# The first layer's projection and its mixing in one stage, part of the conditioning moved to the feed-forward, and one row of the second layer at partition 32

## The reference, cut to what matters

```python
proj = x @ w_in
xa, ba, ca, u, v, xc, da, dg, q, gate = jnp.split(proj, SPLIT_OFFSETS, axis=-1)
y_a = short_gated_conv(xa, ba, ca, conv_a_w)                 # 3 taps
y_b = spatial_gating(u, v, sg_ln_g, sg_ln_b, sg_w, sg_b)     # gelu, layer norm of v, a triangular product over tokens
y_c = multiscale_pool(xc, pool_w, pool_scale)                # trailing means over 2, 4, 8, 16 tokens
y_d = conformer_conv(da, dg, ...)                            # 31 taps, layer norm, silu, a product
y_e = memory_cross_attention(q, mem, w_kv)                   # 4 heads, 256 keys
h = jnp.concatenate([y_a, y_b, y_c, y_d, y_e], axis=-1) * jax.nn.silu(gate)
return h @ w_out
```

## Time and profile before

| what | value |
|---|---|
| median of 3 runs | 2344.21 us (2336.35 to 2350.68) |
| the profiled execution's own time | 2339.87 us |
| its span in the trace | 2338.0 us |
| TensorE, mean granted clock | 0.951 of full |
| TensorE busy | 2187.8 us, 94% |
| VectorE busy | 708.2 us, 30% |
| ScalarE busy | 518.4 us, 22% |
| GpSimd busy | 269.4 us, 12% |

### The profile page before, as it was taken

One profiled execution on the slowest core, in us unless ns is written; L12 is line 12 of the kernel. 1 busy time (PEld: TensorE's weight loads), 2 busy tenths in 40 slices (PEclk: granted clock), 3 DMA queues, 4 the chain that ended last, 5 costly groups with the idle time before them and its releaser, 6 DMA issues. The chain is left out here.

```text
span 2338.0 us, 24977 instructions
## 1 busy us (share of the span) xinstructions
PE 2187.8 (94%) x9866; PEld 1453.9 (62%) x9866; DVE 708.2 (30%) x984; ACT 518.4 (22%) x877; POOL 269.4 (12%) x301
## 2 busy tenths in 40 slices
PE   5999758999999999999999999999999999999992
PEld 3554333665555444444444667675599999999991
DVE  2688631234555200000001366676200000000003
ACT  0000120143432100000001665763112111111110
POOL 2222000200000100000000344443120000000001
PEclk9999868789989999999999999999999999999995
DMA  9887301111110222221321211110196586777863
GB/s 349 307 282 266 137 0 36 36 37 55 54 46 28 72 74 80 74 79 46 121 75 45 64 58 51 55 46 19 67 304 196 185 279 215 247 267 281 297 235 117
DMA packets 81356, 308.66 MB, mean 132 GB/s; under 512 B 9840, under 2 KB 10360, under 8 KB 80992
## 3 DMA queue, kind: packets, MB, share of 16 engines
q1 hardware_dynamic: 60768, 238.05, 30.5%
q0 software_dynamic: 16800, 59.87, 7.2%
q10 hardware_dynamic: 3680, 9.23, 1.1%
HBM read 297.27 MB, written 9.85 MB: 131 GB/s over the span
## 5 line engine op out<-in xcount | busy, mean ns | idle before, releaser
L243 PE MATMUL banks<-sb_x_norm,sb_ring 128*128 128x512 f32 x1344 | 597.3, 604 | 3.9 <-ACT sb_x_norm L385 3.9
L1836 PE MATMUL banks<-sb_act,sb_ring 128*128 128x128 f32 (+3 forms) x4224 | 559.7, 295 | 1.8 <-DVE sb_act L1984 1.0
L1836 PEld LDWEIGHTS banks<-sb_act,sb_ring 128*128 128x128 f32 x4224 | 557.3, 191 | 2.9 <-issue 2.7
L243 PEld LDWEIGHTS banks<-sb_x_norm,sb_ring 128*128 128x128 f32 x1344 | 257.7, 194 | 317.5 <-issue 315.0
L243 PE MATMUL banks<-sb_x_res,sb_ring 128*128 128x512 f32 x448 | 198.7, 603 | 0.0
L1984 DVE TENSOR_TENSOR sb_act<-sb_work,banks 128x128 f32<-128x128 f32 (+3 forms) x88 | 27.7, 315 | 527.4 <-PE banks L1836 527.4
L243 PE MATMUL banks<-sb_act,sb_ring 128*128 128x512 f32 x352 | 153.0, 598 | 3.4 <-PEq L1219 3.4
L243 PEld LDWEIGHTS banks<-sb_x_res,sb_ring 128*128 128x128 f32 x448 | 85.5, 193 | 102.9 <-issue 102.9
L243 PEld LDWEIGHTS banks<-sb_act,sb_ring 128*128 128x128 f32 x352 | 67.5, 192 | 88.9 <-issue 88.9
L538 DVE SCALAR_TENSOR_TENSOR sb_x_norm<-sb_work,sb_cond,sb_x_norm 128x1024 f32<-128x1024 f32 x84 | 107.9, 1284 | 41.2 <-DMA sb_work<-in_cond_w 39.5
L254 PEld LDWEIGHTS banks<-sb_ring,sb_x_norm 128*128 128x128 f32 x1024 | 116.0, 192 | 2.5 <-issue 2.4
(11 more groups left out here) (326 smaller groups left out, 1791.9 us busy)
## 6 DMA issues: line engine op xcount, KB each, us to landing
sb_ring<-in_w_moe_up SPq DMA_DIRECT2D x176, 512.0 KB, 4.5
sb_work<-in_cond_w POOLq DMA_DIRECT2D x96, 512.0 KB, 5.5
sb_ring<-in_w_moe_down SPq DMA_DIRECT2D x64, 704.0 KB, 5.7
sb_ring<-in_w_ffn_up SPq DMA_DIRECT2D x44, 512.0 KB, 3.6
sb_ring<-in_w_h_in SPq DMA_DIRECT2D x32, 512.0 KB, 3.6
sb_ring<-in_w_in SPq DMA_DIRECT2D x28, 512.0 KB, 6.9
sb_ring<-in_w_m_in SPq DMA_DIRECT2D x24, 512.0 KB, 3.6
sb_ring<-in_w_ffn_down SPq DMA_DIRECT2D x16, 704.0 KB, 4.1
```

What stands on the lines that cost most here:

```text
L243: last = m.nc.tensor.matmul(bank[:, 0:act.shape[2]], w[:, rows(k, P)], act[:, k, :], start=(k == 0), stop=(k == kt - 1))
L1836: last = nc.tensor.matmul(ps[:, b % BANKS, 0:cap], m.ring[:, s, rows(k, P)], act, start=(k == 0), stop=(k == kt - 1))
```

## The change

1. `stage_project` and `stage_mix` become `stage_first`. The order of the 28 blocks is DA, DGT, Q, V, U, XC, XA, BA, CA, and the ten gates last. The projection uses two banks in turn (0 and 1); the mixing's products have banks 2 to 6 and stand between the blocks, in an order written out by hand for each engine. Heads are taken in pairs on the two halves of the partitions, and each head of a pair has its own banks and probability tiles. The mixing results go to `W` ungated, and VectorE multiplies each by its gate at the end.
2. Of the twelve conditioning groups, VectorE sums the first, and GpSimd sums groups 1 to 4, with a multiplication and an add per chunk; before, it only issued their loads. The sums of all five go to bank 7. Groups 5 to 11 move to `stage_ffn`: GpSimd issues 56 chunk loads, VectorE adds three chunks after each pair (its loop is unrolled), and TensorE sums over partitions for all seven groups behind the 44 blocks. What the second layers' norm and router need is finished there.
3. In `stage_m` the negated maximum goes to partitions 32 to 39, with a second copy of `sel` there (one more transfer in the setup). `spread_max` of the next head is issued directly behind `spread_floor`, when the exponentials of the present head are done, instead of at the next head's start behind its weights.
4. The masking of `sgw` and the packing of `gates_w` on GpSimd move to the start of `stage_first`.

```diff
@@ Chip.__init__ @@
-        self.sel = sb("sel", [HEADS, HEADS, P])
+        self.sel = sb("sel", [32 + HEADS, HEADS, P])
...
@@ stage_first, replaces stage_project and stage_mix @@
+def spread_group(m, sums, bank, c):
+
+    for j in range(COND // P):
+        last = m.nc.tensor.matmul(m.ps[:, bank, c * 8 + j:c * 8 + j + 1], sums[:, rows(j, P)], m.ones[:, 0:1],
+                                  start=True, stop=True)
+    return last
...
+        @block.gpsimd
...
+            load(0)
+            load(1)
+            pool.wait_ge(m.blocks_done, kv.done + kv.n)
+            load(2)
+            load(3)
+            for n in range(CHUNKS, KD + CHUNKS):
+                pool.wait_ge(chunk_used, n - CHUNKS + 1)
+                load(n)
+            for c in range(1, EARLY_GROUPS):
+                if c >= 2:
+                    pool.wait_ge(acc_done, c - 1)
+                for k in range(KD):
+                    n = c * KD + k
+                    pool.wait_ge(chunk_in[n % CHUNKS], 16 * (n // CHUNKS + 1))
+                    src, total, w = chunk[n % CHUNKS], sums[c % 2], m.cond[:, k:k + 1]
+                    if k == 0:
+                        step(nc.gpsimd.tensor_scalar(total, src, w, None, ALU.mult))
+                    else:
+                        step(nc.gpsimd.tensor_scalar(src, src, w, None, ALU.mult))
+                        step(nc.gpsimd.tensor_tensor(total, total, src, ALU.add))
+                    if n + CHUNKS < EARLY_GROUPS * KD:
+                        load(n + CHUNKS)
+                pool.sem_inc(acc_ready, 1)
...
+            def project(name):
+                b = at[name]
+                s = b % SLOTS
+                pe.wait_ge(m.loaded[s], 16 * (inn.uses[s] + b // SLOTS + 1))
+                pe.wait_ge(m.evac, inn.done + b - 1)
+                by_feature(ps[:, b % 2, :], m.ring[:, s, :]).then_inc(m.blocks_done, 1)
...
+                spread_group(m, sums[c % 2], 7, c).then_inc(acc_done, 1)
...
+            def scores(j):
+
+                pe.wait_ge(m.evac, out_of(Q + 1))
+                if j:
+                    pe.wait_ge(pt_out, 2 * j)
+                for t in range(ST):
+                    for i in range(2):
+                        lo = 64 * i
+                        last = nc.tensor.matmul(ps[:, 2 + 2 * i + t // 2, rows(t % 2, MEM)],
+                                                A[lo:lo + 64, Q + j, rows(t, P)], kT[lo:lo + 64, j, :], start=True,
+                                                stop=True)
+                last.then_inc(score, 1)
...
+            for name in (DA, DA + 1, DGT, DGT + 1, Q, Q + 1):
+                project(name)
+            scores(0)
+            project(V)
+            project(V + 1)
+            turn_probs(0)
+            project(U)
+            attend(0)
+            scores(1)
+            project(U + 1)
+            project(XC)
+            turn_probs(1)
+            project(XC + 1)
+            attend(1)
+            norm_v.mean(m, pe)
+            spread_sums(0)
+            spread_sums(1)
+            project(XA)
+            norm_v.var(m, pe)
+            project(XA + 1)
+            project(BA)
+            turn_values()
+            project(BA + 1)
+            gating()
+            pe.wait_ge(conv_done, 1)
+            norm_c.mean(m, pe)
+            project(CA)
+            norm_c.var(m, pe)
+            project(CA + 1)
+            project(GATES[0])
+            pool_groups()
+            spread_sums(2)
+            project(GATES[1])
+            pointwise()
+            for name in GATES[2:6]:
+                project(name)
+            spread_sums(3)
+            for name in GATES[6:]:
+                project(name)
+            spread_sums(4)
...
@@ scalar, its order @@
+            for name in (DA, DA + 1, DGT, DGT + 1, Q, Q + 1):
+                take(name)
+            exps(0)
+            take(V)
+            take(V + 1)
+            take_probs(0)
+            take(U)
+            take_attended(0)
+            exps(1)
+            take(U + 1)
+            take(XC)
+            take_probs(1)
+            take(XC + 1)
+            take_attended(1)
+            norm_v.square(m, act)
+            take(XA)
+            norm_v.root(m, act)
+            take(XA + 1)
+            take(BA)
+            act.wait_ge(vt_ready, 1)
+            give(act, nc.scalar.activation(A[:, 30:32, :], ps[:, 4:6, :], ACT.Copy), vt_out, 1)
+            take(BA + 1)
+            norm_c.square(m, act)
+            take(CA)
+            norm_c.root(m, act)
+            take(CA + 1)
+            take(GATES[0])
...
@@ vector @@
+            for k in range(KD):
+                dve.wait_ge(chunk_in[k % CHUNKS], 16 * (k // CHUNKS + 1))
+                weigh(m, step, chunk[k % CHUNKS], sums[0], k)
+                dve.sem_inc(chunk_used, 1)
+            dve.sem_inc(acc_ready, 1)
+
+            ready(DGT + 1)
+            step(nc.vector.tensor_tensor(h_in, h_in, A[:, DGT:DGT + 2, :], ALU.mult))
             for f in range(2):
-                step(nc.vector.tensor_scalar(m.conv[:, f, :], h[:, f, :], m.p("dw_w", 2 * (TAPS_D - 1) + f),
+                step(nc.vector.tensor_scalar(conv[:, f, :], h_in[:, f, :], m.p("dw_w", 2 * (TAPS_D - 1) + f),
                                              m.p("dw_b", f), ALU.mult, ALU.add))
-            per = -(-(TAPS_D - 1) // (nch - 3))
-            for c in range(3, nch):
-                conditioning(c)
-                taps(1 + per * (c - 3), min(1 + per * (c - 2), TAPS_D))
-
-            ready(XA)
-            x, s, d = A[:, XC:XC + 2, :], W[:, 12:14, :], A[:, 30:32, :]
-
-            def double(out, src, back):
-                step(nc.vector.tensor_copy(out[:, :, :back], src[:, :, :back]))
-                step(nc.vector.tensor_tensor(out[:, :, back:], src[:, :, back:], src[:, :, :S - back], ALU.add))
-
+            taps(1, 9)
+            softmax(0)
+            taps(9, 16)
+            softmax(1)
+            taps(16, TAPS_D - 1)
...
+            norm_v.centre(m, dve)
+            ready(XC + 1)
+            x, s, d = A[:, XC:XC + 2, :], pooled, pool_tmp
...
+            dve.wait_ge(pw_done, 1)
+            step(nc.vector.tensor_copy(y(YD), ps[:, 4:6, :]))
+            dve.wait_ge(pv_out, 2)
+            for name in GATES:
+                ready(name)
+                tile = W[:, name - GATE, :]
+                step(nc.vector.tensor_tensor(tile, tile, A[:, name, :], ALU.mult))
+            dve.wait_ge(acc_done, EARLY_GROUPS)
+            finish_conditioning(m, step, 0, EARLY_GROUPS, ps[:, 7, 0:8 * EARLY_GROUPS],
+                                ((0, 0, "norm1"), (0, 1, "norm2")))
...
@@ stage_m @@
+    max_row, sel_max, sel_floor = W[32:32 + HEADS, 15, :], m.sel[32:32 + HEADS], m.sel[0:HEADS]
...
+            def spread_max(h):
+                nc.tensor.matmul(ps[:, 5, :], sel_max[:, h, :], max_row, start=True, stop=True).then_inc(spread, 1)
+
             def spread_floor(h):
                 if h:
                     pe.wait_ge(m.norm_in, norms[h - 1].in_k)
                 else:
                     pe.wait_ge(cT_out, 1)
                     pe.wait_ge(floor_out, 1)
-                nc.tensor.matmul(ps[:, 6, :], m.sel[:, h, :], g["f"], start=True, stop=True).then_inc(floor, 1)
+                    pe.wait_ge(row_out, 1)
+                if h < HEADS - 1:
+                    pe.wait_ge(decay, h + 1)
+                nc.tensor.matmul(ps[:, 6, :], sel_floor[:, h, :], g["f"], start=True, stop=True).then_inc(floor, 1)
+                if h < HEADS - 1:
+                    spread_max(h + 1)
...
-                nc.tensor.matmul(ps[:, 5, :], m.sel[:, h, :], g["t"], start=True, stop=True).then_inc(spread, 1)
+                    spread_max(0)
...
@@ stage_ffn @@
+    late = GROUPS - EARLY_GROUPS
+    chunk = [wide(W[:, 2:4, :]), wide(W[:, 4:6, :])] + [wide(A[:, 24 + 2 * i:26 + 2 * i, :]) for i in range(2)]
+    sums = [wide(W[:, 6 + 2 * i:8 + 2 * i, :]) for i in range(6)] + [wide(A[:, 22:24, :])]
...
+            pe.wait_ge(m.acc_ready, GROUPS)
+            for c in range(late):
+                last = spread_group(m, sums[c], 4, c)
+            last.then_inc(m.acc_done, 1)
+
+        @block.gpsimd
+        def _(pool):
+            for n in range(late * KD):
+                if n >= CHUNKS:
+                    pool.wait_ge(m.chunk_used, KD + n - CHUNKS + 1)
+                pool.dma_start(chunk[n % CHUNKS], m.cond_w[EARLY_GROUPS * KD + n]).then_inc(chunk_in[n % CHUNKS], 16)
...
+            def conditioning(n):
+                c, k = divmod(n, KD)
+                dve.wait_ge(chunk_in[n % CHUNKS], 16 * ((EARLY_GROUPS * KD + n) // CHUNKS + 1))
+                weigh(m, step, chunk[n % CHUNKS], sums[c], k)
+                dve.sem_inc(m.chunk_used, 1)
+                if k == KD - 1:
+                    dve.sem_inc(m.acc_ready, 1)
+
+            per = -(-late * KD // (plan.n // 2 - 2))
+            for j in range(plan.n // 2):
+                one(j, j % pairs)
```

(5 more changed lines are left out.)

460 lines of the change are left out of this document (226 added, 234 removed).

## The result

The changed kernel takes 2268.66 us (median of 4 runs, 2266.4 to 2269.22) against 2340.28 us (2335.82 to 2350.68) for the kernel before in the same comparison: ratio 0.9686, 95% interval 0.965 to 0.9722. It is 3.1% faster. The forecast was 2316 us, 1% faster; the measured time lies at the very lower end of the range, where the rival of little contention stood.

What follows compares the result with a forecast made beforehand. TensorE was taken to bound the product stage and later stages, a chain through three engines the mixing. From 2339.87 us, -36 - 1 + 0.7 - 7 + 20 = -23 gave 2316 us, range 2268 to 2333.

Steps and rivals of the forecast that it cites:

- the rival of little contention: Merged stage: GpSimd's multiplication leaves VectorE alone, or the chip arbitrates finer; -79 in the stage, 2273 us, chance 0.22.
- the waits: Merged stage: TensorE waits for VectorE and GpSimd, 0.7 + 18.3 + 4.2 + 21.2 = 44.4 us.
- The merged stage: First layer's product and mixing stages in one: output product starts at 332.4 instead of 368.39, -36 us.
- the second layer: Moved spread_max runs beside spread_floor, saving 1.05 us in seven heads: -7 us, bounds 0 and -20.
- The clock: Merged stage: three restarts at 2.1 us and two falls among the mixing pieces, together 12 us, range 4 to 18.
- TensorE's work: Merged stage: blocks 192.3, five spreads 9.0 and mixing 31 total 232.3 us without any wait.
- the mixing: Merged stage: TensorE's mixing work at full clock, 31 us, with 2.6 taken off for array halves side by side.
- The feed-forward: One-column records behind its product 18 us, VectorE's small operations and a scan 2.5, chunk loads and adds hidden: +20 us.
- The output product: Product behind the merged stage: weights stream in as before, it may keep the clock, -1 us (0 to -2).
- the setup: Kernel's start: one more DMA issue on ScalarE's queue, +0.7 us (0 to 1).
- A cheap multiplication: Merged stage: GpSimd's multiplication costs 1.28 us for 1024 columns, waits shrink to 19; 2291 us, chance 0.07.
- GpSimd ending the stage: Merged stage: GpSimd's 1024-column operations cost 1.3 times the line, last spread waits 21 us; 2355 us, chance 0.07.

Runs made afterwards that it cites:

- c1_mult_broadcast: Changed kernel with GpSimd's multiplication by a column written as a product of two tensors, the second a broadcast column: 2297.74 us, ratio 0.9816.
- a1_no_sums: Changed kernel without GpSimd's arithmetic from the second chunk of each group on, loads and waits kept: 2243.37 us, ratio 0.9577.
- c2_sums_on_vector: Changed kernel with VectorE adding all forty chunks instead of GpSimd, normed values ahead of pooling, spreads where their group is due: 2244.71 us, ratio 0.9598.

## Why the prediction was right and wrong

**The step that failed** is this premise: "an operation of GpSimd is let through between two of VectorE, and VectorE's next one waits until it has ended", applied to the multiplication too ("Nothing shows it for GpSimd's multiplication by a column, the longer one; I assume the same"). It holds for GpSimd's operations that read two tensors: an add of 2.35 us makes a tap 2.72. The multiplication by a column lets VectorE go after some 0.9 of its 2.85 us. With that, four taps pass in a chunk's 6.4 us, 16 taps take 25.5 us, and the waits are 20.4 us instead of 44.4. The merged stage was missed by 35.1 us (-71.1 against -36); 24.0 of them are these waits, and `c1_mult_broadcast`, where the premise holds for both operations, brings 19.7 of them back. Of the whole miss of some 50 us, the second layer has another 10.2 and the third layer's two falls 3.9.

The Trainium skill has both halves of the rule. Trainium Architecture — The Big Picture, What this means for kernel authors, calls the shared port pair of VectorE and GpSimd "an exclusive lock (not a bandwidth split)"; the trace agrees for the adds, behind whose end the held tap finishes (2.72 us for 0.75). Beside a multiplication a tap takes 1.48 us, and the trace does not tell a short stop from a slower run. The Trainium skill's GPSIMD Engine Reference, Key points, names VectorE's instructions with two SBUF inputs, or in a 2-port mode, as those that contend; the taps read two tensors, and the trace agrees, but the runs add that it depends on GpSimd's operation how long they suffer (1.48 us for a tap beside a multiplication, 2.71 beside a product of two tensors).

**The clock**, 12 us by the prediction, cost 4.6. TensorE's records behind the two waits in the changed kernel, and the transposes of `turn_values` in `a1_no_sums`, which does not wait there:

```profile
107.08 1.97 PE L621 MATMUL banks<-sb_cst,sb_act 128*128 128x128 f32 x8 [7.91 <-DVE sb_act L811]
110.43 1.97 PE L621 MATMUL banks<-sb_cst,sb_act 128*128 128x128 f32 x8 [1.38 <-DVE sb_act L811]
112.19 8.21 PE L243 MATMUL banks<-sb_x_res,sb_ring 128*128 128x512 f32 x16
...
186.80 1.97 PE L640 MATMUL banks<-sb_cst,sb_act 128*128 128x128 f32 x8 [10.38 <-DVE sb_act L861]
188.56 7.58 PE L243 MATMUL banks<-sb_x_res,sb_ring 128*128 128x512 f32 x16
```

```profile
166.44 1.04 PE L637 MATMUL banks<-sb_cst,sb_act 128*128 128x128 f32 x8
```

The transposes take twice their time (2.0 us lost in the sixteen ahead of the first block, 0.9 in the eight ahead of the second) and the blocks 8.2 and 7.6 us for 7.0 (1.2 and 0.6 lost). A restart thus cost 2.3 us in the mean, close to the 2.1 of the prediction; there were two instead of three, and no mixing piece made the clock fall in this kernel. In the kernel with waits of 15, 7 and 17 us the stage's mean granted clock was 0.93 instead of 0.96.

**TensorE's work**, 232.3 us without waits by the prediction, is 228.0: in `c2_sums_on_vector`, where the clock is 1.00 throughout, the stretch is 232.0 us with 4.0 us of waits. That the stretches without GpSimd's arithmetic last 232.3 and 232.0 us with their waits is chance. What was too dear is **the mixing**, 26 us at full clock by the starts of its rows, not 31: the halves of the array do work side by side (16 records of scores in 2.00 us, 8 of attending in 1.94, where 0.43 us for 512 columns makes 3.4), which saves 6 us where 2.6 were taken, and the transposes and the gating take 6.3 us instead of 8. The sum of the miss is 24.0 (waits) + 7.4 (clock) + 4.3 (work) = 35.7 us for the 35.1.

**The second layer** was the other mis-sized term: -7, measured -17.2 (-13.2 for the edit alone in the kernel before, with one fall left). The bound of -20, with the four clock falls gone as well, was named, and not taken. The seven pairs saved the 7.4 us that were said of them, but the wait for the exponentials, which was to cost nothing, took 2.1 of it back in three heads; the rest, 11.9 us, is the falls'.

**The feed-forward**, +20, was right in sum (+19.3), with two terms that cancel. The one-column records took 20.5 us (18 forecast). The small operations, 2.5 by estimate, cost nothing: the gap ahead of the down product is 3.1 us, against 3.4 before, because they stand where VectorE's last product stood, and that one now runs under the one-column records. The chunks' loads and adds were hidden, as said. **The output product** (-1) and **the setup** (+0.7) were within 1.3 us.

**The rivals.** Little contention was forecast at 2273 with a chance of 0.22, and the time came out there, but only its first sentence holds, that the multiplication leaves VectorE alone, and that in part: the time landed at 2268 because the second layer gave 10 us more, while 20.4 us of waits remained where this rival had 4.5. That the whole time agrees with this rival is luck. A cheap multiplication is out (2.85 us). GpSimd ending the stage did not occur, but the margin was 0.1 us; the break-even factor of 1.2 belonged to a stage with 44 us of waits in it, which left GpSimd more time.

## What to carry to other kernels

Before moving arithmetic to GpSimd beside a busy VectorE, look at how many tensors GpSimd's operation reads: here those with two stopped VectorE's two-tensor operations for their whole length, the multiplication of one by a column for a third of it, so that a form that is faster by itself (1.91 for 2.85 us) made the stage longer by 22.6 us. Then ask whether VectorE was short of time at all: here it could take the same sums in 41 us of its idle time, for which GpSimd was busy for 182 us, its issues of loads included. And where a trace shows a clock fall behind narrow matmuls, price each fall separately (some 4 us here) and ask of every edit near it how many it removes, before counting the microseconds of the matmuls.

## What the runs showed of the hardware

- GpSimd, 128x1024 f32: multiplication by a column 2.85 us, add 2.35, product with a broadcast column 1.91, a third less than the first.
- A tap of VectorE (a multiply-add of about 512 columns that reads two tensors) beside them: 1.48 to 2.03, 2.72 and 2.71 to 2.78 us, for 0.75 alone; beside a 512-column multiplication 1.06, beside a 512-column add 1.63.
- Two matmuls with 8 rows each, at partitions 0 and 32, ran interleaved: four records in 1.06 us, where the same pair at one partition took 1.91.
- The clock of TensorE fell in 6 of 8 heads of the second layer in one kernel and in 4 in another, with the same matmuls in that layer. What in the rest of the kernel makes the difference is not shown.
